# Two in-projection chunks between the opening's transposes, and the recurrent result kept in the decay buffer

## The chip, the cores and the metric

The kernel runs on one core of a Trainium2 chip. A core has a matrix engine (PE), a vector engine (DVE), a scalar engine (ACT), GpSimd (POOL) and SP, which here only issues transfers. ACT issues transfers too. Each engine works through its own instructions in order and waits on semaphores for the others. PE writes to PSUM, which has 8 banks of 512 float32 for each of 128 partitions. The metric is the device time of one execution in microseconds; lower is better.

## What is computed

One inference step of a hybrid decoder layer: 2048 prompt rows with 16 learned rows ahead of them, and 8 sample rows with a paged cache. Both groups go through

```python
h = rmsnorm(x, norm_mix)
q, k, v, f_logit, xr, gr = split(h @ w_in)          # 512, 512, 512, 8, 512, 512 columns
att = forgetting_attention(q, k, v, log_sigmoid(f_logit + b_forget))
rnn = linear_recurrence(conv4(xr), gates) * gelu(gr)
x = x + concat(rmsnorm(att), rmsnorm(rnn)) @ w_out
x = x + (gelu(conv3(g)) * val) @ w_ffn_down          # g, val = split(rmsnorm(x) @ w_ffn_up)
y = rmsnorm(x)
```

The change touches the first two lines and the order in time of the fourth. All arithmetic stays as it is.

## The kernel before, in words

The 2072 rows, padded to 2080, stand along the free dimension: activations are kept transposed. Products of full precision are made of three passes, high part by high part, high by low and low by high.

**The opening** takes 17 tiles of 128 rows (the last has 32). SP loads a tile into `xin[:, t % 2]` (L467). ACT takes the mean square (`mean_square`, L876 and L878). DVE scales the tile into `hn[:, t % 2]` (`normalise`, L1306 and L1308). PE transposes both, eight 128 x 128 pieces of the raw tile and eight of the normalised one (`turn`, L1838), into four banks; even tiles have banks 0 to 3, odd ones 4 to 7. ACT copies the raw half to `xst`, the normalised half to `XH` (`empty`, L886 and L887) and stores `xst` to `xT` in DRAM (L889). DVE subtracts to get the low part `XL` (`low`, L1315). Then small vector and scalar work on recurrent constants (L1351 to L1366) runs before `g_ev` is raised by 5, for which the first projection waits.

The semaphores of the opening: `x_tp` counts tiles transposed, `x_ev` evictions by ACT (two a tile), `x_sq` mean squares, `x_hn` normalised tiles, `x_lo` low parts. The load of tile t + 2 waits for `x_tp` of tile t, since it takes the same `xin` slot. The order on DVE is `normalise(t + 1)`, `low(t)`.

**The projections** take 21 chunks of 128 output columns: weights `WR` (SP, L477) are split by POOL into `WH` and `WL` (`split_w`, L706 and L708), and PE makes, per chunk, five blocks of 416 rows (`project`, L1857), block j into bank j, of 8 x 3 = 24 matmuls. DVE copies a bank to `ZS[:, j]` (`empty_block`, L1371) and ACT stores it (`store_block`, L918). Chunks 0 to 7 are xr and gr in turn, in four passes of a loop; chunk 8 holds the forget logits; then four groups of q, k and v follow, two in each pass of a loop over i.

**The recurrent branch** runs beside each group c of q, k and v. ACT loads `RX` from `xrT` (L985) once the previous store of `RX` to `mixT` has landed (`r_st`). DVE makes the convolution into `RC` between the evictions of q (L1448 to L1463); PE needs it for the gate products in chunk k (L1928, L1929). ACT writes the decay `RA` by block, DVE scans into `RW`, and the result of the group goes to `RX` (L1505), from where it is stored (L1040).

## Time and profile before

| | us |
|---|---|
| median of 3 runs | 3661.2 |
| range of the 3 runs | 3655.61 to 3663.19 |
| span of the profiled execution | 3658.3 |
| opening, to the first projection matmul | 110.07 |
| projections, to about | 690 |

The profile gives no device time of its own execution beside the span, so the span stands for it; it lies within the range of the three runs. In the page, a row of the chain says what the end was waiting for, followed backwards; a timeline row is start, duration, engine, line, what is written from what; "xN" merges N instructions. PE is the chain's engine in most of the span, so idle time of other engines costs nothing unless PE waits for them.

### The profile page before, as it was taken

To read this page: it belongs to the slowest core of one execution; us is meant where nothing else is said; L and a number is where in the kernel's file an instruction comes from. 1 tells how busy PE (TensorE), PEld (TensorE's weight loads), DVE (VectorE), ACT (ScalarE), POOL (GpSimd) and SP (SyncE) were. 2 spreads that over 40 slices of the span, in tenths; PEclk is the share of its full clock that TensorE was granted. 3 is DMA by queue.
4 is the path that set the end of the run, shared out by engine and by line. 5 is a ranking of instruction groups with operands and counts; after the bars stand their busy time and mean duration, and the time that the engine had idled before them with its cause. 6 is when DMAs were issued, how large, how long until landed. Compare 5 with 4: busy or idle time off the path is not lost.

```text
span 3658.3 us, 47526 instructions
## 1 busy us (share of the span) xinstructions
PE 3277.7 (90%) x15540; PEld 2765.0 (76%) x15540; DVE 1544.5 (42%) x1934; ACT 743.8 (20%) x1226; POOL 1024.5 (28%) x443
## 2 busy tenths in 40 slices
PE   4898989677898898999689899999999997999998
PEld 4898888543344444444589899999999997999998
DVE  4213333387656765672431644444444443112220
ACT  5000222321122122222300400000000002333332
POOL 1111111141332333230432622222222221444443
PEclk8999999767889988999899999999999998999999
DMA  5212444547565755563423311111111113544553
GB/s 186 77 70 64 100 93 97 109 105 203 172 175 172 211 153 163 165 197 94 127 95 124 116 47 46 46 46 46 49 46 46 46 41 124 168 162 164 189 180 108
DMA packets 254855, 422.68 MB, mean 116 GB/s; under 512 B 48545, under 2 KB 158730, under 8 KB 250554
## 3 DMA queue, kind: packets, MB, share of 16 engines
q1 hardware_dynamic: 168466, 326.84, 30.0%
q10 hardware_dynamic: 85936, 92.82, 8.4%
q8 instruction: 76, 1.25, 0.1%
q14 instruction: 89, 0.73, 0.1%
q0 software_dynamic: 288, 1.05, 0.1%
HBM read 337.35 MB, written 83.40 MB: 115 GB/s over the span
## 4 chain that ended last, share of the span: by engine, by line
PE 69%; DVE 8%; DMA 7%; issue 6%; SPq 4%; POOL 4%; ACT 2%; DVEq 0%; ACTq 0%; POOLq 0%
PE PS L2105 32%; PE PS L1857 12%; PE PS L2033 4%; PE PS L2044 3%; PE PS L2188 3%; PE PS L2190 3%; PE PS L2189 3%; DMA Kpg<-in_cache_k 2%; SPq L509 2%; DMA GR<-gT 2%; SPq L510 1%; PE PS L1956 1%; PE PS L2017 1%; DVE prod L1563 1%; POOL ML L835 1%
## 5 line engine op out<-in xcount | busy, mean ns | idle before, releaser
L2105 PE MATMUL PS<-MH,VH 128*128 128x416 f32 x2080 | 738.3, 355 | 35.9 <-issue 27.0
L2105 PE MATMUL PS<-MH,VL 128*128 128x416 f32 x2080 | 732.1, 352 | 0.0
L2105 PE MATMUL PS<-ML,VH 128*128 128x416 f32 x2080 | 732.0, 352 | 0.0
L2105 PEld LDWEIGHTS PS<-MH,VH 128*128 128x128 f32 x2080 | 392.8, 189 | 44.0 <-issue 27.9
L2105 PEld LDWEIGHTS PS<-ML,VH 128*128 128x128 f32 x2080 | 393.9, 189 | 3.8
L2105 PEld LDWEIGHTS PS<-MH,VL 128*128 128x128 f32 x2080 | 392.7, 189 | 5.1
L2033 PE MATMUL PS<-PT,VA 128*128 128x416 f32 (+16 forms) x816 | 354.3, 518 | 14.6 <-ACT PT L1097 13.3
L2188 PE MATMUL PS<-GH,DH 128*128 128x416 f32 x880 | 320.2, 364 | 46.9 <-POOL DL L860 28.5
L823 POOL TENSOR_TENSOR VR<-VR,gains 128x1024 f32<-128x1024 f32 x52 | 98.7, 1899 | 927.9 <-PE PS L2105 808.0
L860 POOL TENSOR_TENSOR DL<-DR,DH 128x1408 fp32r<-128x1408 f32 x80 | 258.3, 3229 | 353.3 <-ACT DH L1220 353.1
L1097 ACT ACTIVATE PT<-PS 128x416 f32<-128x416 f32 (+16 forms) x408 | 187.2, 460 | 718.4 <-PE PS L2019 501.6
L1956 PE MATMUL PS<-KA,QA 68*128 68x512 f32 (+3 forms) x360 | 218.3, 630 | 121.5 <-DVE MP L1524 89.8
L1857 PE MATMUL PS<-XH,WH 128*128 128x416 f32 x840 | 307.1, 366 | 19.2 <-issue 11.2
L2190 PE MATMUL PS<-GH,DL 128*128 128x416 f32 x880 | 313.6, 356 | 0.0
L2189 PE MATMUL PS<-GL,DH 128*128 128x416 f32 x880 | 313.4, 356 | 0.0
L1857 PE MATMUL PS<-XH,WL 128*128 128x416 f32 x840 | 296.9, 353 | 0.0
L1857 PE MATMUL PS<-XL,WH 128*128 128x416 f32 x840 | 296.4, 353 | 0.0
L1524 DVE TENSOR_REDUCE MP<-PS 128x1 f32<-128x512 f32 (+3 forms) x360 | 208.1, 601 | 132.7 <-PE PS L1956 96.8
L2044 PE MATMUL PS<-Vpg,sc 128*8 128x512 f32 x512 | 254.9, 622 | 3.4 <-DMA Vpg<-in_cache_v 3.1
L1766 DVE COPY GP<-PS 128x416 f32<-128x416 f32 x110 | 64.9, 592 | 423.0 <-PE PS L2105 422.6
L767 POOL TENSOR_TENSOR prod<-Kpg,qb 128x1024 f32<-128x1024 f32 x56 | 132.7, 2370 | 367.9 <-DMA Kpg<-in_cache_k 267.0
L1186 ACT ACTIVATE GC<-GC 128x416 f32<-128x416 f32 x110 | 60.8, 552 | 841.2 <-DVE GC L1738 754.1
(238 smaller groups left out, 4702.0 us busy)
## 6 DMA issues: line engine op xcount, KB each, us to landing
Kpg<-in_cache_k SPq DMA_DIRECT2D x256, 256.0 KB, 3.0
Vpg<-in_cache_v SPq DMA_DIRECT2D x256, 256.0 KB, 3.0
DR<-in_w_down SPq DMA_DIRECT2D x80, 704.0 KB, 4.1
gT<-GO ACTq DMA_DIRECT2D x110, 208.0 KB, 1.9
GR<-gT SPq DMA_DIRECT2D x55, 416.0 KB, 5.1
VR<-in_w_up SPq DMA_DIRECT2D x44, 512.0 KB, 3.5
Kst<-kT SPq DMA_DIRECT2D x24, 520.0 KB
WR<-in_w_stream SPq DMA_DIRECT2D x21, 512.0 KB, 3.5
```

Of the source, the lines that this page charges most:

```text
L767: e.tensor_tensor(prod[:, g % 2], Kpg[:, g % 4], qb[:, v].unsqueeze(1).to_broadcast([P, 2, DATT]), ALU.mult).then_inc(kpp, 1)
L860: e.tensor_tensor(DL[:, h], DR[:, h], DH[:, h].bitcast(F32), ALU.subtract).then_inc(d_lo, 1)
L1097: e.activation(PT[0:kr, t % 3, 0:n], PS[0:kr, (u + t) % 2, 0:n], ACT.Exp, scale=0.125).then_inc(ex, 1)
L1524: e.tensor_reduce(MP[0:rows, qt, pc:pc + 1], PS[0:rows, 2 + p % 2, 0:n], AX.X, ALU.max).then_inc(mx, 1)
L1857: mm = e.matmul(PS[:, j, 0:BW], w[:, u, k], x[:, k, cols(j)], start=(k == 0 and q == 0), stop=(k == KC - 1 and q == 2))
L1956: mm = e.matmul(o[:, 0:n], QA[0:HD + 4, v, qt * P:qt * P + rows], KA[0:HD + 4, v, k0:k0 + n], start=True, stop=not diag)
L2033: e.matmul(PS[:, 4 + (u + j) % 2, o:o + n], VA[0:kr, u, kt], PT[0:kr, t % 3, 0:n], start=(kt == 0), stop=t in ENDS).then_inc(pv, 1)
L2044: mm = e.matmul(PS[0:NH, 7, :], sc[:, u, 2 * g + m, :], Vpg[:, g % 4, m], start=(g == 0 and m == 0), stop=False)
L2105: mm = e.matmul(PS[:, j, 0:BW], w[:, u, k], x[:, k, cols(j)], start=(k == 0 and q == 0), stop=(k == KC - 1 and q == 2))
L2188: e.matmul(PS[:, v, 0:BW], DH[:, h, k], GH[:, r, m], start=(kk == 0), stop=False)
L2189: e.matmul(PS[:, v, 0:BW], DH[:, h, k], GL[:, r, m], start=False, stop=False)
L2190: e.matmul(PS[:, v, 0:BW], DL[:, h, k], GH[:, r, m], start=False, stop=(kk == FC - 1))\
```

## The change

The opening is written out as a list, `OPENING`: tiles 0 to 16, with ten units of work between and after them. A unit is one block of chunk 0 (even k) or chunk 1 (odd k), block j = k // 2. Units 0 and 1 follow tiles 4 and 5, units 2 and 3 tiles 7 and 8, and so on; units 8 and 9 follow tile 16. Units use banks 0 to 3 in turn, so every tile's raw transposes go to banks 4 and 5 and the normalised ones to banks 6 and 7; `x_tp` now counts halves. SP stores the units' blocks. The rest of the projections starts with chunk 2. `ZS` moves to an address of its own. In the recurrent branch the result is written over the decay `RA` and stored from there; the load of `RX` waits for the previous result to be computed, and the first write of `RA` in a group for the store to have landed.

```diff
@@ -162,6 +162,26 @@
     return plan
 
 
+def opening():
+
+    ready = {4: 0, 7: 1, 10: 2, 13: 3, 16: 4}
+    found, due = [], []
+    for t in range(NT):
+        found.append(("tile", t))
+        if due:
+            found.append(("unit", due.pop(0)))
+        if t in ready:
+            found.append(("unit", 2 * ready[t]))
+            due.append(2 * ready[t] + 1)
+    return found + [("unit", k) for k in due]
+
+
+def tiles_for(k):
+
+    return min(NT, ((k // 2 + 1) * BW + P - 1) // P)
+
+
+OPENING = opening()
 PLANS = [attention_plan(True, False), attention_plan(False, False), attention_plan(False, True)]
 
 
...
@@ -461,17 +481,25 @@
             e.dma_start(xin[:, 1], a["x_prompt"][0][P - NMETA:2 * P - NMETA, :]).then_inc(x_ld[1], 16)
             for u in range(2):
                 e.dma_start(WR[:, u], a["w_stream"][u]).then_inc(w_ld[u], 16)
-            with e.Fori(0, 7) as i:
-                for v in range(2):
-                    e.wait_ge(x_tp, 2 * i + v + 1)
-                    e.dma_start(xin[:, v], a["x_prompt"][0][bass.ds((2 * i + 2 + v) * P - NMETA, P), :])\
-                        .then_inc(x_ld[v], 16)
-            e.wait_ge(x_pad, 1)
-            e.dma_start(xin[0:NMETA, 0], a["x_prompt"][0][SEQ - NMETA:SEQ, :]).then_inc(x_ld[0], 16)
-            e.dma_start(xin[NMETA:NMETA + NS, 0], a["x_sample"][:, 0, :]).then_inc(x_last, 16)
-
-
-            with e.Fori(1, 10) as i:
+            for what, n in OPENING:
+                if what == "tile" and n < NT - 3:
+                    e.wait_ge(x_tp, 2 * n + 2)
+                    e.dma_start(xin[:, n % 2], a["x_prompt"][0][(n + 2) * P - NMETA:(n + 3) * P - NMETA, :])\
+                        .then_inc(x_ld[n % 2], 16)
+                if what == "tile" and n < 2:
+                    e.wait_ge(w_lo, n + 1)
+                    e.dma_start(WR[:, n], a["w_stream"][2 + n]).then_inc(w_ld[n], 16)
+                if what == "tile" and n == NT - 3:
+                    e.wait_ge(x_pad, 1)
+                    e.dma_start(xin[0:NMETA, 0], a["x_prompt"][0][SEQ - NMETA:SEQ, :]).then_inc(x_ld[0], 16)
+                    e.dma_start(xin[NMETA:NMETA + NS, 0], a["x_sample"][:, 0, :]).then_inc(x_last, 16)
+                if what == "unit":
+                    j = n // 2
+                    e.wait_ge(g_ev, 5 + n + 1)
+                    e.dma_start((xrT if n % 2 == 0 else grT)[0:P, cols(j)], ZS[:, n % NB]).then_inc(z_st[n % NB], 16)
+
+
+            with e.Fori(2, 10) as i:
                 for u in range(2):
                     e.wait_ge(w_lo, 2 * i + u - 1)
                     e.dma_start(WR[:, u], a["w_stream"][2 * i + u]).then_inc(w_ld[u], 16)
...
@@ -700,7 +728,9 @@
             def split_w(n, use, u):
 
                 e.wait_ge(w_ld[u], 16 * use + 16)
-                if not (isinstance(n, int) and n < 2):
+                if isinstance(n, int) and n in (2, 3):
+                    e.wait_ge(g_mm, n + 7)
+                elif not (isinstance(n, int) and n < 2):
                     e.wait_ge(g_mm, 5 * n - 5)
                 e.sem_inc(go, 1)
                 e.tensor_copy(WH[:, u], WR[:, u]).then_inc(w_hi, 1)
...
@@ -879,14 +911,15 @@
                              scale=1.0 / DM).then_inc(x_sq, 1)
 
             def empty(t, u, st, rows=P):
-                e.wait_ge(x_tp, t + 1)
+                e.wait_ge(x_tp, 2 * t + 1)
                 e.wait_ge(x_st[u], st + 1)
-                raw = PS[:, 4 * u:4 * u + 2, :].rearrange("p a (k n) -> p (a k) n", n=P)
-                nrm = PS[:, 4 * u + 2:4 * u + 4, :].rearrange("p a (k n) -> p (a k) n", n=P)
+                raw = PS[:, 4:6, :].rearrange("p a (k n) -> p (a k) n", n=P)
+                nrm = PS[:, 6:8, :].rearrange("p a (k n) -> p (a k) n", n=P)
                 e.activation(xst[:, u, :, 0:rows], raw[:, :, 0:rows], ACT.Copy).then_inc(x_ev, 1)
-                e.activation(XH[:, :, bass.ds(t * P, rows)], nrm[:, :, 0:rows], ACT.Copy).then_inc(x_ev, 1)
+                e.wait_ge(x_tp, 2 * t + 2)
+                e.activation(XH[:, :, t * P:t * P + rows], nrm[:, :, 0:rows], ACT.Copy).then_inc(x_ev, 1)
                 e.wait_ge(x_ev, 2 * t + 1)
-                e.dma_start(xT.rearrange("(k p) n -> p k n", p=P)[:, :, bass.ds(t * P, rows)],
+                e.dma_start(xT.rearrange("(k p) n -> p k n", p=P)[:, :, t * P:t * P + rows],
                             xst[:, u, :, 0:rows]).then_inc(x_st[u], 16)
 
             e.wait_ge(c_pool, 3)
@@ -894,18 +927,15 @@
             mean_square(0, 0, 16)
             mean_square(1, 1, 16)
             empty(0, 0, 0)
-            with e.Fori(0, 7) as i:
-                act0.start(i, 2)
-                for v in range(2):
-                    e.wait_ge(x_hn, 2 * i + v + 1)
-                    mean_square(2 * i + 2 + v, v, 16 * i + 32)
-                    empty(2 * i + 1 + v, 1 - v, 16 * (i + v))
-                act0.stop(7)
-            e.wait_ge(x_last, 16)
-            e.wait_ge(x_hn, 15)
-            mean_square(16, 0, 16 * 9, TAIL)
-            empty(15, 1, 16 * 7)
-            empty(16, 0, 16 * 8, TAIL)
+            for t in range(1, NT):
+                if t + 1 < NT:
+                    e.wait_ge(x_hn, t)
+                    if t + 1 == NT - 1:
+                        e.wait_ge(x_last, 16)
+                        mean_square(t + 1, 0, 16 * 9, TAIL)
+                    else:
+                        mean_square(t + 1, (t + 1) % 2, 16 * ((t + 1) // 2 + 1))
+                empty(t, t % 2, 16 * (t // 2), P if t < NT - 1 else TAIL)
             e.wait_ge(c_pool, 14)
             e.dma_start(rh0[:, :, 0:NS], a["rnn_h"]).then_inc(c_ld, 16)
 
...
@@ -981,7 +1014,7 @@
-                    e.wait_ge(r_st, 16 * c + 1)
+                    e.wait_ge(r_y, c + 1)
...
@@ -1014,6 +1047,7 @@
+                            e.wait_ge(r_st, 16 * c + 1)
...
@@ -1037,7 +1071,7 @@
-                            e.dma_start(mixT[bass.ds(DATT + c * P, P), :], RX[:, 3:3 + TP]).then_inc(r_st, 16)
+                            e.dma_start(mixT[bass.ds(DATT + c * P, P), :], RA[:]).then_inc(r_st, 16)
...
@@ -1301,8 +1335,8 @@
 
             def normalise(t, u, rows=P):
                 e.wait_ge(x_sq, t + 1)
-                if not (isinstance(t, int) and t < 2):
-                    e.wait_ge(x_tp, t - 1)
+                if t >= 2:
+                    e.wait_ge(x_tp, 2 * t - 2)
                 e.reciprocal(st0[0:rows, u, 2:3], st0[0:rows, u, 1:2]).then_inc(d0, 1)
                 e.wait_ge(d0, t + 1)
                 e.scalar_tensor_tensor(out=hn[0:rows, u], in0=xin[0:rows, u], scalar=st0[0:rows, u, 2:3],
@@ -1310,21 +1344,24 @@
 
             def low(t, u, rows=P):
                 e.wait_ge(x_ev, 2 * t + 2)
-                nrm = PS[:, 4 * u + 2:4 * u + 4, :].rearrange("p a (k n) -> p (a k) n", n=P)
-                c = bass.ds(t * P, rows)
+                nrm = PS[:, 6:8, :].rearrange("p a (k n) -> p (a k) n", n=P)
+                c = slice(t * P, t * P + rows)
                 e.tensor_tensor(XL[:, :, c], nrm[:, :, 0:rows], XH[:, :, c].bitcast(F32),
                                 ALU.subtract).then_inc(x_lo, 1)
 
             normalise(0, 0)
             normalise(1, 1)
-            low(0, 0)
-            with e.Fori(0, 7) as i:
-                for v in range(2):
-                    normalise(2 * i + 2 + v, v)
-                    low(2 * i + 1 + v, 1 - v)
-            normalise(16, 0, TAIL)
-            low(15, 1)
-            low(16, 0, TAIL)
+            e.sem_inc(g_ev, 5)
+            for what, n in OPENING:
+                if what == "tile":
+                    if n + 2 < NT:
+                        normalise(n + 2, n % 2, P if n + 2 < NT - 1 else TAIL)
+                    low(n, n % 2, P if n < NT - 1 else TAIL)
+                else:
+                    e.wait_ge(g_mm, n + 1)
+                    if n >= NB:
+                        e.wait_ge(z_st[n % NB], 16 + 1)
+                    e.tensor_copy(ZS[:, n % NB], PS[:, n % 4, 0:BW]).then_inc(g_ev, 1)
 
             g_steps = Steps(e, dv)
 
...
@@ -1362,15 +1399,15 @@
-            e.wait_ge(x_tp, NT)
+            e.wait_ge(x_tp, 2 * NT)
-            e.sem_inc(g_ev, 5)
-            with e.Fori(0, 4) as c:
+            e.wait_ge(t_pe, 2)
+            with e.Fori(1, 4) as c:
...
@@ -1502,7 +1539,7 @@
-                            e.tensor_tensor(x[:, 3:3 + TP], w[:], r[:], ALU.mult).then_inc(r_y, 1)
+                            e.tensor_tensor(al[:], w[:], r[:], ALU.mult).then_inc(r_y, 1)
...
@@ -1829,25 +1866,43 @@
             e.wait_ge(c_pool, 3)
 
             def turn(t, u, rows=P):
-                e.wait_ge(x_hn, t + 1)
-                if not (isinstance(t, int) and t < 2):
-                    e.wait_ge(x_ev, 2 * t - 2)
-                    e.wait_ge(x_lo, t - 1)
-                for src, b in ((xin, 4 * u), (hn, 4 * u + 2)):
+                for src, b in ((xin, 4), (hn, 6)):
+                    if b == 4 and t:
+                        e.wait_ge(x_ev, 2 * t - 1)
+                    if b == 6:
+                        e.wait_ge(x_hn, t + 1)
+                        if t:
+                            e.wait_ge(x_lo, t)
+                    else:
+                        e.wait_ge(x_sq, t + 1)
                     for k in range(KC):
                         mm = e.transpose(PS[:, b + k // 4, (k % 4) * P:(k % 4) * P + rows],
                                          src[0:rows, u, k * P:(k + 1) * P], identF[0:rows, 0:rows])
-                mm.then_inc(x_tp, 1)
-
-            turn(0, 0)
-            turn(1, 1)
-            with e.Fori(1, 8) as i:
-                for u in range(2):
-                    turn(2 * i + u, u)
-            turn(16, 0, TAIL)
-
-            e.wait_ge(x_ev, 2 * NT)
-            e.wait_ge(x_lo, NT)
+                    mm.then_inc(x_tp, 1)
+
+            def opening_unit(k):
+
+                j, u = k // 2, k % 2
+                tiles = tiles_for(k)
+                e.wait_ge(x_ev, 2 * tiles)
+                e.wait_ge(x_lo, tiles)
+                e.wait_ge(w_lo, u + 1)
+                if k >= 4:
+                    e.wait_ge(g_ev, 5 + k - 3)
+                for c in range(KC):
+                    for q, (w, x) in enumerate(((WH, XH), (WH, XL), (WL, XH))):
+                        mm = e.matmul(PS[:, k % 4, 0:BW], w[:, u, c], x[:, c, cols(j)],
+                                      start=(c == 0 and q == 0), stop=(c == KC - 1 and q == 2))
+                mm.then_inc(g_mm, 1)
+
+            for what, n in OPENING:
+                if what == "tile":
+                    turn(n, n % 2, P if n < NT - 1 else TAIL)
+                else:
+                    opening_unit(n)
+            e.wait_ge(g_ev, 5 + 9)
+            e.transpose(PS[0:TAIL, 5, 0:P], ZS[:, 8 % NB, 3 * P:BW], identF[:]).then_inc(t_pe, 1)
+            e.wait_ge(g_ev, 5 + 10)
 
             def project(n, u, j, hi, lo, w_hi_t, w_lo_t):
 
```

## Rows read from the trace of the kernel before

**Rows 1.** the page, part 4: the chain that ended last, by engine

```profile
PE 69%; DVE 8%; DMA 7%; issue 6%; SPq 4%; POOL 4%; ACT 2%; DVEq 0%; ACTq 0%; POOLq 0%
```

**Rows 2.** chain of waits in order of time, opening: start us, us, what

```profile
18.50 3.67 DMA xin<-in_x_prompt
...
25.52 3.63 PE PS L1838 x16
...
29.34 3.85 DMA xin<-in_x_prompt
```

**Rows 3.** timeline, first tiles: start us, us, engine, line, operation

```profile
14.64 1.94 PE L1838 MATMUL PS<-identF,xin 128*128 128x128 f32 x8 [14.64 <-DVE hn L1308]
...
22.19 1.06 ACT L876 ACTIVATE sqj<-xin 128x1024 f32<-128x1024 f32 x1 [1.92 <-DMA xin<-in_x_prompt]
...
24.00 1.28 DVE L1308 SCALAR_TENSOR_TENSOR hn<-xin,st,gmix 128x1024 f32<-128x1024 f32 x1
24.47 1.01 ACT L887 ACTIVATE XH<-PS 128x1024 f32 x1
...
25.65 1.22 DVE L1315 TENSOR_TENSOR XL<-PS,XH 128x1024 f32 x1 [0.37 <-ACT XH L887]
...
29.85 1.04 PE L1838 MATMUL PS<-identF,hn 128*128 128x128 f32 x8
```

**Rows 4.** timeline, the last two tiles

```profile
94.38 0.95 POOL L713 MEMSET xin<- 32x1024 f32 x1 [75.69 <-PE PS L1838]
...
98.17 1.05 ACT L876 ACTIVATE sqj<-xin 32x1024 f32<-32x1024 f32 x1 [1.79 <-DMA xin<-in_x_sample]
...
103.43 0.38 ACT L887 ACTIVATE XH<-PS 128x256 fp32r<-128x256 f32 x1
...
103.84 0.42 DVE L1315 TENSOR_TENSOR XL<-PS,XH 128x256 fp32r<-128x256 f32 x1 [1.12 <-ACT XH L887]
```

**Rows 5.** timeline, matmuls 1 and 13 of the first projection block

```profile
110.07 0.72 PE L1857 MATMUL PS<-XH,WH 128*128 128x416 f32 x1 [6.96 <-DVEq L1367]
...
114.35 0.35 PE L1857 MATMUL PS<-XH,WH 128*128 128x416 f32 x1
```

**Rows 6.** chain of waits in order of time, projections and recurrent branch

```profile
184.98 45.32 PE PS L1857 x240
...
415.76 14.97 DMA mixT<-RX
430.89 5.66 DMA RX<-xrT
```

**Rows 7.** timeline around the first recurrent boundary

```profile
407.37 0.59 DVE L1371 COPY ZS<-PS 128x416 f32<-128x416 f32 x1
...
414.59 2.40 POOL L708 TENSOR_TENSOR WL<-WR,WH 128x1024 fp32r<-128x1024 f32 x1
...
418.86 0.53 ACTq L971 DMA_DIRECT2D out_v_sample<-TS  x1
```

**Rows 8.** windows: stretch, its length, engines' busy us, PEclk, DMA share, GB/s

```profile
37.00:48.00 11.00, 6.76 (x34) 6.53 (x34) 5.45 (x7) 6.05 (x10) 0.00 (x0) 0.66 0.63 193
...
429.00:431.00 2.00, 1.00 1.00 389
431.00:433.00 2.00, 1.00 0.95 264
433.00:435.00 2.00, 1.00 1.04 438
```

**Rows 9.** PE's waits at the three boundaries: total us, times, longest

```profile
PE PS L1921 <- DVE ZS L1371: 7.4, 1, 7.4
...
PE PS L1857 <- issue: 11.2, 1, 11.2
...
PE PS L1921 <- DVE ZS L1371: 5.6, 1, 5.6
```

**Rows 10.** the instructions on xin: their transfers, issue to landing

```profile
DMA to landing us min/median/max: 2.0/4.0/5.1
```

More of the change, by code:

```diff
@@ L216, in build @@
         WL = sb("WL", [P, 2, KC, P], F32R, m1)
+        ZS = sb("ZS", [P, NB, BW], F32, m1)
         m0 = ExitStack()
@@ L224, in build @@
         m0.close()
-        ZS = sb("ZS", [P, NB, BW], F32, m1)
         TS = sb("TS", [P, 2, 4, P], F32, m1)
@@ L711, in _ @@
             split_w(1, 0, 1)
-            e.wait_ge(x_tp, 15)
+            e.wait_ge(x_tp, 30)
             e.memset(xin[0:TAIL, 0], 0.0).then_inc(x_pad, 1)
@@ L717, in _ @@
             e.wait_ge(x_ev, 2 * NT)
+            split_w(2, 1, 0)
             e.wait_ge(x_st[0], 16 * 9 + 1)
@@ L720, in _ @@
             e.memset(gw[:], 0.0).then_inc(c_gw, 1)
-            with e.Fori(1, 10) as i:
+            split_w(3, 1, 1)
+            with e.Fori(2, 10) as i:
                 for u in range(2):
@@ L925, in take_tail @@
                 e.wait_ge(t_ev, ev + 2)
-            with e.Fori(0, 4) as c:
+            take_tail(0, 0, 0)
+            e.dma_start(out["rnn_conv_prompt"][0, 0][:, 0:P], TS[NMETA - 3:NMETA, 0, 0]).then_inc(t_st[0], 16)
+            e.dma_start(out["rnn_conv_sample"][0][:, 2, 0:P], TS[NMETA:NMETA + NS, 0, 0]).then_inc(t_st[0], 16)
+            with e.Fori(1, 4) as c:
                 for j in range(NB):
@@ L1371, in empty_block @@
                 return e.tensor_copy(ZS[:, j], PS[:, j, 0:BW]).then_inc(g_ev, 1)
-            with e.Fori(0, 4) as c:
+            e.wait_ge(t_pe, 2)
+            with e.Fori(1, 4) as c:
                 for u in range(2):
@@ L1866, in chunk @@
                         after(j)
-            with e.Fori(0, 4) as c:
+            with e.Fori(1, 4) as c:
                 chunk(2 * c, 0)
```

## The prediction

> **What bounds the kernel now.** I began with the page: the chain that ended last lies on the matrix engine (PE) for 69% of the span [rows 1]. PE work that is neither added nor removed can only be moved, so what the change can win is PE's idle time near the edited places. I then read the chain of waits in order of time over the opening [rows 2] and the timeline of two of its tiles [rows 3]. The reader should see a loop two tiles long: PE transposes both tiles (3.6 to 3.7 us), the next input load starts 0.2 us after that and takes 3.67 and 3.85 us, squares and the normalised copy follow, and 10.84 us after the one load the next of its kind starts (18.50, 29.34). The transposes of seventeen tiles end at about 103.1, just before the last evictions [rows 4]. Then small vector work holds the first matmul until 110.07 [rows 5]. Third, I read the projection stage: 240 matmuls in 45.32 us with no gap [rows 6], and at the recurrent branch's boundaries the chain and the waits [rows 6, 9].
>
> **Part 1, the moved projections.** Chunks 0 and 1 are ten units of 24 matmuls, 45.32 us by a later pair [rows 6], so 4.53 us each. The first 12 intervals from 110.07 take 4.28 us [rows 5] against 12 x 0.19 = 2.3 later, so the pair ends and chunk 2 starts at about 110.07 + 45.3 + 2.0 = 157.4 today. That moment is what I compare. If the opening kept its pace, eight of the ten units would vanish into it, with the 7 us of small vector work.
>
> It does not keep it. The edit gives units the four lower banks, so all tiles share one pair of banks for raw and one for normalised transposes. PE's normalised half of tile t now waits for `low(t-1)` (x_lo >= t). On the vector queue `low(t-1)` is now written behind `normalise(t+1)`. That waits for tile t+1's square on the scalar engine, hence for its load, and the load waits for both halves of tile t-1 on PE. In the old order two tiles shared each turn of that circle. Now each tile goes round alone:
> - end of PE's half to start of the square: 0.19 (29.15 to 29.34), a load of 3.8, the mean of seven such in the chain, of which two stand in [rows 2]: 3.98 us;
> - start of the square to end of the normalised copy: 22.19 to 25.28, 3.09 us [rows 3];
> - `low`: 1.22 us, and 0.1 us until PE starts [rows 3];
> - eight normalised transposes: 1.04 us at the full clock, 1.9 us at the lower level, as after the pauses of some 5 us [rows 3].
>
> That is 9.43 us per tile at the full clock (warm), 10.30 at the lower (cold), in place of 10.9 / 2 = 5.45. The raw half is off this circle: it only needs the previous raw eviction.
>
> What the units cost: unit and raw half take 4.53 + 1.04 = 5.6 us, up to 7.6 where 2.0 us of slow start come in, and PE has 8.39 us in each circle until `low` is done. So they are hidden. After a unit the pause is under 3 us and I take the next half as warm; after a tile with no unit the pause is some 6 us and I take it as cold, like [rows 3]. Tiles 5, 6, 8, 9, 11, 12 and 14 are then warm, and 1 to 4, 7, 10, 13 cold.
>
> The moved queue work: the ten block stores go from the scalar queue to SP's, each issued before the next input load. Their wait (eviction, behind `low`) ends while PE does its half, so the issue delays the load by nearly nothing, but 208 KB stand in front of it; at 389 to 438 GB/s [rows 8] that is 0.5 us, for seven of the loads. Two weight loads move into tiles 0 and 1, 512 KB beside input loads: 0.5 us once. The scalar order (square of t+1, then evictions of t) hides its evictions behind the load. Vector evictions of units (0.59 us [rows 7]) fall between `low` and the next square's arrival.
>
> The sum of times: the first normalised half starts at 14.64 and takes 1.9, so tile 0 ends at 16.6. Tile 1: + 10.3 + 0.5 = 27.4. Tiles 2 to 4: + 30.9 = 58.3. Tiles 5 to 14: 7 x 9.43 + 3 x 10.30 = 96.9, and 7 x 0.5 for stores: 158.7. Tile 15 waits for the short last load by way of the pad: 94.33 to 98.17 is 3.84 [rows 4], the copy's end 3.0 later, `low` and PE 2.36: 167.9. Tile 16 needs only the eviction and `low` of tile 15: 0.15 + 1.02 + 0.1 + 1.22 + 0.1 + 1.04 = 3.6, 171.5. Its own eviction and `low`, 0.38 + 0.42 with the gaps 0.9 [rows 4], free unit 8 at 172.4. Units 8 and 9: 9.1; the last eviction and its signals 0.8: chunk 2 starts at 182.3. Its weights (split once unit 8 is done at 177: 2.40 us for the low part [rows 7] and under 2 for the high) are ready by 181. Against 157.4 this is a **loss of 24.9 us**. The small vector work of 3.7 us follows beside chunk 2, whose first eviction is due 4.5 us after its start, at no cost.
>
> Bounds: the circle's load has 3.67 us at least in the chain and 5.1 at most to landing [rows 2, 10]: -2 to +15 us over 14 circles. All halves warm: -6; all cold: +6. If a unit ran at the slow pace throughout (24 x 0.35 by [rows 5], + 1.94 for the raw half = 10.3 us), it would overrun 8.39 by 2.0, over eight units and the last two +24. No cost of the stores: -4.
>
> Here a rule speaks against my sum. What the row shows is two tiles of transposes back to back, 3.63 us, for one wait for a load [rows 2]. The Trainium skill (TensorE: Matmul & The Clock Gate, "HAM oscillation — how this bites in real kernels") reports that double-buffering PSUM gave no further gain to one kernel; by that, losing it costs nothing, and the time is that of the rival "kept pace" below.
>
> **Part 2, the recurrent result in the decay buffer.** Today the load of RX waits until the store of RX to mixT has landed: 14.97 us, then 5.66 us [rows 6]. PE stands 7.4 us at the first such boundary and 5.6 at the third, for evictions that stand behind the convolution, which needs RX [rows 9]. At the second PE stands for 11.2 us in "issue" [rows 9], which is no wait for RX, and no stall for RX follows: nothing to win. After the change the load is issued at about 419.4, behind the last value rows [rows 7], but on the same queue behind the same 1040 KB store. I take it as running after the store at the window's pace, mean of 389, 264 and 438 = 364 GB/s [rows 8]: 1.065 MB in 2.9 us, landing at 433.7 in place of 436.5. That saves 2.8 us; twice, **5.6 us**. Bounds: nothing, if the store is slowed by what the load takes; or the whole 7.4 + 5.6 = 13.0 us, if the load passes the store. I stay near the low end since store and load are equal in bytes and share the engines. The Trainium skill (DMA: Bandwidth & Descriptors, "Queues, rings and completion order") says each engine takes a queue's descriptors in ring order; the sum would be the same. The new wait, that the decay buffer's store has landed before the next exponentials, stands on the scalar queue ahead of everything behind it, but those exponentials need the convolution, so RX, which lands after the store even in the sum above: free.
>
> **Total.** 3658.3 + 24.9 - 5.6 = 3677.6 for the span; the median of the runs shown is 2.9 above this span, so 3680.5 us.
>
> **The rivals.**
> - *Kept pace* (faster). If `normalise(t+1)` were ready before PE ends tile t-1's half, the circle would be open and the opening would end at 103.1 as now. Unit 8 would start at 104.0, and chunk 2 at 104.0 + 9.1 + 0.8 = 113.9: 43.5 + 5.6 = 49 us less, 3612. It decides from the point at which load, square and copy (7.1 us) fit into one tile's period of 5.45; the load alone takes 3.67 or more after PE [rows 2], which speaks against it. For it speaks only that the lower bound of each term is not proven in the new rhythm.
> - *Light circle* (no change). Loads at 3.67 (-4), all halves warm (-6), no cost of stores (-4), and RX passing the store (-7.4): 3680.5 - 21 = 3659. Each is possible; together they are rare.
> - *Units not hidden* (slower still). PE pauses in every circle, and the granted clock in the opening is 0.66 at 37 to 48 [rows 8]. If units run at the lower level, 24 us more: 3704.
> - *The change does nothing for RX*, as ring order and slowed store cancel: 3686; inside the forecast's range.
>
> **How the numbers follow.** Circle per tile with units hidden, 0.72 (its own range 3668 to 3698); units not hidden or instruction fetch in the long unrolled code 0.12; light circle 0.09; kept pace 0.07. Leaving out kept pace and the far ends, the range is 3664 to 3704. 0.2% is 7.3 us, about what a measurement of this kernel can tell from no change. Faster 0.08; same 0.10 (light circle and the low tail of the forecast); slower 0.82.
>
> **What would show it.** Right: PE's groups of eight normalised transposes about 9.5 to 10.3 us apart, input loads issued singly at that spacing, `low` starting at the end of the normalised copy of the tile two ahead, unit 9 ending near 181, and the RX load landing near the store's landing plus 3. Wrong, if tiles follow at 5.5 us (the circle is open), if a unit and raw half last over 8.4 us, or if RX lands before 430 and PE's boundary stalls vanish.

## The result

| | before | after |
|---|---|---|
| median of the runs (5 each), us | 3662.91 | 3684.69 |
| range of the runs, us | 3655.61 to 3666.07 | 3674.43 to 3688.69 |
| span of the profiled execution, us | 3658.3 | 3682.9 |
| ratio after to before, 95% interval | | 1.0054 (1.0037 to 1.007) |

The changed kernel is slower by 0.54%, or 21.8 us between the medians; the spans differ by 24.6 us. The forecast was 3680.5 in a range of 3664 to 3704. To see whether it was right for its reasons, the same eight places of both traces are set against each other. Each is the start of the same piece of work, or the landing of the same transfer.

| place | before | after | difference | forecast |
|---|---|---|---|---|
| tile 14's halves done on PE | – | 161.0 | – | 158.7 |
| chunk 2 starts | 157.5 | 187.65 | +30.1 | +24.9 |
| last projection evicted, POOL writes Kst | 690.1 | 724.4 | +34.3 | +19.3 |
| first Kst load landed | 720.1 | 755.0 | +34.9 | +19.3 |
| first block of attention's output, AO | 788.9 | 824.5 | +35.6 | +19.3 |
| last block of attention's output, AO | 1760.0 | 1787.3 | +27.3 | +19.3 |
| first load of the down product | 3066.3 | 3093.9 | +27.6 | +19.3 |
| end of the span | 3658.3 | 3682.9 | +24.6 | +19.3 |

The loss is older than the attention stage: it is +30 where the projections go on with chunk 2, a little more at their end, and some 10 less at the end of the span. So two questions stand open: why the recurrent part gave nothing of its 5.6 us, and where these 10 us came back from, in stages that the change doesn't touch.

The page of after, part 4, answers [rows 1]; the chain is by engine:

```profile
PE 64%; issue 10%; DVE 8%; DMA 6%; SPq 5%; POOL 4%; ACT 2%; ACTq 0%; DVEq 0%; POOLq 0%
```

PE has fallen from 69% to 64% of the chain and "issue" has risen from 6% to 10%. The rise is a single piece, in the chain of the opening of after (start us, us, what):

```profile
18.76 142.25 issue
```

This chain runs back from the last input load to the pad that POOL writes into `xin` before it, and from there along POOL's own queue, where 142.25 us, 3.9% of the span, read as "issue". By the waits POOL stood for PE all that time. So the shares of the chain say little about the opening, and the waits say more. Over the first 190 us of after (columns: engine, line, waited for, us in total, times, longest) the rows of POOL, DVE and PE are:

```profile
POOL xin L743 <- PE PS L1879: 142.3, 1, 142.3
DVE st L1340 <- ACT st L910: 121.6, 16, 11.6
...
PE PS L1879 <- DVE XL L1349: 74.2, 16, 7.7
```

In all sixteen tiles after the first PE waits for the low part of the tile before, 74.2 us together. Before, the transposes waited on the scalar engine's eviction in seven places and for `hn` in four.

The timeline of one turn in after (columns as in [rows 3]), from one normalised half to the next:

```profile
56.80 1.94 PE L1879 MATMUL PS<-identF,hn 128*128 128x128 f32 x8 [7.01 <-DVE XL L1349]
...
58.77 0.33 SPq L487 DMA_DIRECT2D xin<-in_x_prompt  x1
...
62.86 1.06 ACT L908 ACTIVATE sqj<-xin 128x1024 f32<-128x1024 f32 x1 [3.07 <-DMA xin<-in_x_prompt]
...
63.63 1.03 PE L1879 MATMUL PS<-identF,xin 128*128 128x128 f32 x8
...
64.57 1.29 DVE L1342 SCALAR_TENSOR_TENSOR hn<-xin,st,gmix 128x1024 f32<-128x1024 f32 x1
...
65.78 1.22 DVE L1349 TENSOR_TENSOR XL<-PS,XH 128x1024 fp32r<-128x1024 f32 x1
66.91 0.58 DVE L1364 COPY ZS<-PS 128x416 f32<-128x416 f32 x1
67.14 1.06 PE L1879 MATMUL PS<-identF,hn 128*128 128x128 f32 x8 [2.47 <-DVE XL L1349]
67.52 0.35 SPq L499 DMA_DIRECT2D xrT<-ZS  x1
...
68.23 0.33 SPq L487 DMA_DIRECT2D xin<-in_x_prompt  x1
```

Read it downwards. PE ends tile 4's half at 58.74 and the load of tile 6 goes out at once. The unit and tile 5's raw half fill PE until 64.66. The load lands, the square starts at 62.86, the normalised copy of tile 6 ends at 65.86, and only then does `low` of tile 4 run, although its data had lain ready since ACT's eviction ended at 59.8. PE's next half starts 0.14 us after `low`, at 67.14: 10.34 us after the last one. Over the whole opening the normalised halves of tiles 0 and 16 start at 14.63 and 173.82, 9.95 us per tile; before it was 5.45.

The end of the opening, chain of waits of after (start us, us, what):

```profile
162.36 2.73 DMA xin<-in_x_sample
...
175.83 10.86 PE PS L1894 x48
...
187.65 27.43 PE PS L1912 x144
```

### The profile page after: what moved, and what is told of

Same layout as the page of the kernel before. It is cut to its first block, busy times and chain, and to the rows that moved or that the text cites. A ratio compares the mean times of both kernels' runs of the same rounds, so it can differ in the third digit from the quotient of the medians.

```text
span 3682.9 us, 47256 instructions
## 1 busy us (share of the span) xinstructions
PE 3268.0 (89%) x15540; PEld 2759.3 (75%) x15540; DVE 1548.0 (42%) x1934; ACT 744.9 (20%) x1226; POOL 1025.2 (28%) x443
## 4 chain that ended last, share of the span: by engine, by line
PE 64%; issue 10%; DVE 8%; DMA 6%; SPq 5%; POOL 4%; ACT 2%; ACTq 0%; DVEq 0%; POOLq 0%
PE PS L2160 31%; PE PS L1912 10%; PE PS L2099 3%; PE PS L2088 3%; PE PS L2243 3%; PE PS L2245 3%; PE PS L2244 3%; DMA GR<-gT 2%; DMA Kpg<-in_cache_k 2%; SPq L537 2%; SPq L538 1%; DVE prod L1600 1%; PE PS L2011 1%; DVE MP L1561 1%; POOL ML L867 1%
## 5 line engine op out<-in xcount | busy, mean ns | idle before, releaser
L2243 PE MATMUL PS<-GH,DH 128*128 128x416 f32 x880 | 320.1, 364 | 44.1 <-POOL DL L892 26.5
L1912 PE MATMUL PS<-XH,WH 128*128 128x416 f32 x760 | 278.2, 366 | 14.1 <-issue 12.2
L1912 PE MATMUL PS<-XH,WL 128*128 128x416 f32 x760 | 268.1, 353 | 0.0
L1912 PE MATMUL PS<-XL,WH 128*128 128x416 f32 x760 | 267.9, 352 | 0.0
```

The lines of the kernel that those rows point to most:

```text
L1912: mm = e.matmul(PS[:, j, 0:BW], w[:, u, k], x[:, k, cols(j)], start=(k == 0 and q == 0), stop=(k == KC - 1 and q == 2))
L2243: e.matmul(PS[:, v, 0:BW], DH[:, h, k], GH[:, r, m], start=(kk == 0), stop=False)
```

## The experiments

All ratios are against runs of the kernel before on the same chip. Two theories about the opening stood against each other: the circle of the prediction, in which `low` stands behind `normalise` of the tile two ahead, and a cost of the single banks, the units or the instructions themselves. About the recurrent part there were two as well: the load gains its 2.8 us each time, or it gains nothing because the wait for the store never was what held it.

### One part at a time (e1, e2)

The changed kernel with the four edits of the recurrent branch taken back (e1, shown), and the kernel before with the same four made (e2, the reverse of these lines):

```diff
-                    e.wait_ge(r_y, c + 1)
+                    e.wait_ge(r_st, 16 * c + 1)
...
-                            e.wait_ge(r_st, 16 * c + 1)
...
-                            e.dma_start(mixT[bass.ds(DATT + c * P, P), :], RA[:]).then_inc(r_st, 16)
+                            e.dma_start(mixT[bass.ds(DATT + c * P, P), :], RX[:, 3:3 + TP]).then_inc(r_st, 16)
...
-                            e.tensor_tensor(al[:], w[:], r[:], ALU.mult).then_inc(r_y, 1)
+                            e.tensor_tensor(x[:, 3:3 + TP], w[:], r[:], ALU.mult).then_inc(r_y, 1)
```

> The changed kernel with its recurrent part taken back: RX is again loaded after the store of RX has landed; the new opening stays. In the trace of the changed kernel RX lands 20.9 us after the store to mixT is issued, against 20.8 before. Theory (the circle of one tile in the opening is the whole loss, the recurrent part brings nothing): the time of the changed kernel, 3685 us within 4. Rival (the recurrent part saves its 5.6 us and something else in that run ate them): about 3690 us.

Measured: 3684.05 us, ratio 1.0083 (1.006 to 1.0106).

> The kernel before with the recurrent part of the change alone. Theory (no gain, as RX still lands about 21 us after the store is issued and PE still stands 7.4 us at the first boundary): 3663 us, ratio 1.000. My recorded step (load right behind the store, 2.8 us at two boundaries): 3657 us, ratio 0.9985. If the load passed the store: 3650 us.

Measured: 3659.96 us, ratio 1.0013 (0.9999 to 1.0028). The opening alone carries the whole loss, and the recurrent part alone saves nothing: the 5.6 us of the forecast would be a ratio of 0.9985, which lies below the interval of e2. Against its own runs of before, though, e1 is 27.7 us slower and the whole change 21.8. That gap of 5.9 us is as large as the saving that was forecast; the two intervals overlap, so e1 by itself can't tell the theories apart. The chain of waits shows what became of the load. First the opening alone, where load follows store as in [rows 6], then the recurrent part alone:

```profile
445.29 14.64 DMA mixT<-RX
...
460.10 6.13 DMA RX<-xrT
```

```profile
420.34 15.16 DMA RX<-xrT
```

The wait for the store has gone from the chain, and the load, issued about 10 us earlier than in [rows 6], lasts 15.16 us instead of 5.66. It lands at 435.5, before at 436.55.

### The order of two instructions on the vector queue (e3)

The changed kernel, with `low` written ahead of `normalise` in the opening. Nothing else differs, banks and units least of all.

```diff
                 if what == "tile":
+                    low(n, n % 2, P if n < NT - 1 else TAIL)
                     if n + 2 < NT:
                         normalise(n + 2, n % 2, P if n + 2 < NT - 1 else TAIL)
-                    low(n, n % 2, P if n < NT - 1 else TAIL)
```

> The changed kernel with one edit: on the vector queue low(n) stands before normalise(n + 2) instead of behind it. Theory (that order closes the circle of 9.4 to 10.4 us per tile): the circle is open, a tile takes about 5 us, 6.6 with a unit on PE (4.53 + 2 x 1.04), so chunk 2 starts near 120 instead of 187.6 and the time is 3615 to 3625 us. Rival (single-banked PSUM or the transfers set the pace, whatever the vector order): tiles stay near 10 us and the time near 3685 us; one between them, if the single banks cost a part.

Measured: 3621.78 us, ratio 0.99 (0.9876 to 0.9924); chunk 2 starts at 127.60. That is 60 us earlier than in after and 30 earlier than before. In the waits over the first 190 us the row that stood at 74.2 has shrunk, and in the timeline `low` now starts well before the next normalised copy:

```profile
PE PS L1879 <- DVE XL L1349: 8.3, 10, 1.6
```

```profile
61.49 1.23 DVE L1349 TENSOR_TENSOR XL<-PS,XH 128x1024 fp32r<-128x1024 f32 x1 [0.34 <-ACT XH L920]
...
62.86 1.06 PE L1879 MATMUL PS<-identF,hn 128*128 128x128 f32 x8 [0.16 <-DVE XL L1349]
63.05 1.28 DVE L1342 SCALAR_TENSOR_TENSOR hn<-xin,st,gmix 128x1024 f32<-128x1024 f32 x1
```

The normalised halves of tiles 0 and 16 now start at 14.5 and 114.15: 6.2 us per tile, units included. PE now waits in seven places for the eviction of the raw half instead, 12.3 us in all. So the single banks by themselves cost at most the 0.8 us per tile between 6.2 and the 5.45 of before, with eight units inside; the order in which DVE takes two operations cost some 60 us. The chain of this kernel shows what is late next, the input loads on their own:

```profile
53.95 4.12 DMA xin<-in_x_prompt
...
65.26 4.70 DMA xin<-in_x_prompt
```

Of the 60 us that chunk 2 gained against after, the total shows the whole: e1, with the opening of after, took 3684.05 us on the same chip, 62.3 more.

### All units after the last tile (e4)

```diff
-    ready = {4: 0, 7: 1, 10: 2, 13: 3, 16: 4}
...
-    return found + [("unit", k) for k in due]
+    return [("tile", t) for t in range(NT)] + [("unit", k) for k in range(10)]
```

> The changed kernel with all ten units after tile 16 instead of eight of them between tiles. Theory (eight units are wholly hidden in PE's wait of 8.4 us in each circle): their 8 x 4.53 = 36 us come back, some 4 us for colder transposes are added and some 4 us of store cost saved: 3721 us. Rival (units are not hidden but lengthen the circles): nothing changes or little, 3685 to 3700 us.

Measured: 3715.09 us, ratio 1.0162 (1.0137 to 1.0187). Waits of PE over the first 190 us, and the chain:

```profile
PE PS L1870 <- DVE XL L1340: 104.9, 16, 7.4
```

```profile
177.18 48.03 PE PS L1885 x240
...
226.19 27.44 PE PS L1903 x144
```

Without units between the tiles, tile 16 is done at nearly the same time (the first unit starts 1.35 us later, 177.18 against 175.83), and chunk 2 starts 38.5 us later than in after (226.19 against 187.65). Eight units are 36 us of that. So in the circle they did cost nothing, as forecast: PE simply stood 30.7 us longer for the same sixteen low parts. The rival by which units were not hidden falls. The total shows 31.0 us of the 38.5 (3715.09 against 3684.05 of e1, on the same chip).

### The low part twice (e5)

`low` of tiles 0 to 14 is computed a second time into a scratch tile, before the real one; the wait of `normalise` is counted accordingly. This lengthens one link of the circle by a known amount and nothing else.

```diff
+                if t < NT - 2:
+                    e.tensor_tensor(dup[:], nrm, XH[:, :, c].bitcast(F32), ALU.subtract).then_inc(d0, 1)
                 e.tensor_tensor(XL[:, :, c], nrm[:, :, 0:rows], XH[:, :, c].bitcast(F32),
                                 ALU.subtract).then_inc(x_lo, 1)
```

> The changed kernel with every low part of tiles 0 to 14 computed twice (the first copy into a scratch tile; no result of the kernel depends on it). Theory (low stands in a circle that every tile goes round alone): each of 15 circles grows by one such operation, 1.13 to 1.22 us, so 17 to 18 us more than the changed kernel, about 3702 us against 3685. Rival (low is covered by the load or by PE's transposes and units): the changed kernel's time, 3685 us.

Measured: 3705.91 us, ratio 1.0112 (1.009 to 1.0135). Timeline of one turn, and the start of chunk 2 in the chain:

```profile
47.24 1.22 DVE L1351 TENSOR_TENSOR dup<-PS,XH 128x1024 fp32r<-128x1024 f32 x1
48.38 1.22 DVE L1352 TENSOR_TENSOR XL<-PS,XH 128x1024 fp32r<-128x1024 f32 x1
```

```profile
207.81 27.43 PE PS L1915 x144
```

Fifteen doubled operations of 1.14 us (48.38 less 47.24) are 17.1 us; chunk 2 came 20.2 us later, and the median is 21.2 above that of after. The 3 us beyond the 17.1 are not traced; two traces with the same opening, after and e1, have chunk 2 start 1.8 us apart (187.65 and 185.86). DVE is busy for 42% of the span of after, and yet what is put on this one operation arrives in full at the end. That is what it is to lie on the circle.

### What holds the load of RX (e6)

In the trace of after the store goes out at 447.11, the load at 453.39. The DMA queue of ACT around them (timeline), and the windows (stretch, length, then PE, PEld, DVE, ACT and POOL busy us, PEclk, DMA share, GB/s):

```profile
443.18 0.39 ACTq L1070 DMA_DIRECT2D out_rnn_h_sample<-RW  x1
...
447.11 0.76 ACTq L1074 DMA_DIRECT2D mixT<-RA  x1
...
453.39 3.71 ACTq L1018 DMA_DIRECT2D RX<-xrT  x1
```

```profile
453.00:455.00 2.00, 2.00 (x13) 1.98 (x12) 0.00 (x0) 0.00 (x0) 0.00 (x0) 1.00 1.67 51
...
461.00:463.00 2.00, 2.00 (x12) 1.98 (x12) 0.00 (x0) 0.00 (x0) 0.00 (x0) 1.00 0.98 401
```

For 12 us after the store's issue hardly anything moves: at 453 to 455 the share of the engines is 1.67, and yet they move only 51 GB/s, where at 461 to 463 a share of 0.98 moves 401. Then 1.06 MB of store, 1.06 MB of load and 0.52 MB of weights go at about 400 GB/s. The packets of three windows of after, 443 to 445, 453 to 455 and 461 to 463:

```profile
DMA packets 1236, 0.02 MB, mean 11 GB/s; under 512 B 1201, under 2 KB 1236, under 8 KB 1236
...
DMA packets 21, 0.10 MB, mean 51 GB/s; under 512 B 3, under 2 KB 9, under 8 KB 9
...
DMA packets 227, 0.80 MB, mean 401 GB/s; under 512 B 17, under 2 KB 83, under 8 KB 185
```

The share of 1.67 is not made of small pieces: it is 21 packets, most of them large, which last 2.5 us each (1.67 x 16 engines x 2 us over 21), where the 227 later ones last 0.14. The small pieces came before. Some 1200 packets start at 443 to 445, and they belong to two transfers issued ahead of the store: the last column of `RW` (prompt) and eight columns (samples) go to DRAM as 128 x 9 = 1152 elements of 4 bytes each. Between them and the store two transfers of value rows are issued, which are the other candidates. They stay as they are in what follows.

To test it the recurrent state is stored another way. PE transposes the nine columns into bank 6, ACT copies them, and they go out as nine rows of 512 bytes. The edit is made on the kernel before, with neither part of the change; the computed result is the same. It changes the place in the queue as well as the size of the pieces: the state now goes out behind the store to `mixT` and directly ahead of the load of `RX`.

```diff
+                        if j == 3:
+                            e.wait_ge(r_sc, c + 1)
+                            e.transpose(PS[0:1 + NS, 6, 0:P], RW[:, TPR - 1:TPR + NS], identF[:]).then_inc(x_pad, 1)
...
-                            e.dma_start(out["rnn_h_prompt"][0].rearrange("o n -> n o")[bass.ds(c * P, P), :],
-                                        RW[:, TPR - 1:TPR]).then_inc(r_ho, 16)
...
+                    e.activation(HR[0:1 + NS], PS[0:1 + NS, 6, 0:P], ACT.Copy).then_inc(d0, 1)
...
+                    e.dma_start(out["rnn_h_prompt"][0][:, bass.ds(c * P, P)], HR[0:1]).then_inc(r_ho, 16)
+                    e.dma_start(out["rnn_h_sample"][0][:, bass.ds(c * P, P)], HR[1:1 + NS]).then_inc(r_ho, 16)
```

> The kernel before, where the recurrent state is transposed on PE (one transpose a group, into bank 6) and stored as nine rows of 512 bytes, instead of 1152 elements of 4 bytes each. Theory (these small writes stand ahead of the store to mixT on the scalar queue and hold it for 10 of its 15 us, and hold instruction fetch at the second boundary): the store lands in about 5 us, RX in about 5 more, PE's stalls of 7.4, 11.2 and 5.6 us shrink to 0 to 3 each: 15 to 24 us faster than the kernel before, some 3637 us, ratio 0.9935 to 0.996. Rival (the store takes 15 us by itself, or by the value rows around it): 3658 us, ratio 1.000.

Measured: 3607.22 us, ratio 0.985 (0.9833 to 0.9867). The transfers around the first boundary, 410 to 440, in the trace of before and then in this kernel's (tiles, queue, KB each, us from issue to landing; ahead of them the packets by size):

```profile
DMA packets 3426, 3.60 MB, mean 120 GB/s; under 512 B 1672, under 2 KB 3040, under 8 KB 3168
...
mixT<-RX ACTq DMA_DIRECT2D x1, 1040.0 KB, 15.0
RX<-xrT ACTq DMA_DIRECT2D x1, 1040.0 KB, 5.7
WR<-in_w_stream SPq DMA_DIRECT2D x1, 512.0 KB, 16.7
```

```profile
DMA packets 2692, 4.24 MB, mean 141 GB/s; under 512 B 545, under 2 KB 2306, under 8 KB 2434
...
mixT<-RX ACTq DMA_DIRECT2D x1, 1040.0 KB, 4.4
RX<-xrT ACTq DMA_DIRECT2D x1, 1040.0 KB, 5.8
...
WR<-in_w_stream SPq DMA_DIRECT2D x1, 512.0 KB, 5.2
```

Some 1100 small packets are gone from the window, and with them 10.6 us of the store and 11.5 us of a weight load on another queue. So the 15 us of the "store" [rows 6] were 4.4 us of store and 10.6 us for which 4.5 KB ahead of it held it up. The place alone doesn't explain it: the nine rows now stand directly ahead of the load of `RX`, which took 5.8 us, as against 5.7. Whether the 4-byte writes, moved behind the store as they are, would have done less harm was not tried. This is the step that the prediction had wrong: the load of RX was not waiting for a store, both were waiting for what went before. PE's waits between 400 and 760, first the longest of before (its other two, for ZS and in "issue", stand in [rows 9]), then those with the rows:

```profile
PE PS L1956 <- POOL QA L743: 31.3, 1, 31.3
```

```profile
PE PS L1961 <- POOL QA L744: 22.2, 1, 22.2
...
PE PS L1857 <- issue: 3.4, 1, 3.4
```

The two stalls for ZS, 7.4 and 5.6 us, have gone; the one in "issue" has shrunk by 7.8 us, and the wait for the first load of attention by 9.1 (Kst lasts 12.55 us in the chain in place of 21.58). The projections end at 663.6, not 690.1; the stalls are 20.8 us of these 26.5, and much of the rest is PE's slow start behind them, as in the 29.98 us for the 144 matmuls after the second stall of before, against 27.44 for as many in e3 (from 127.60). The expectation was a gain of 0.4 to 0.65%; it was 1.5%. Of the 49 us between the two spans, 35.6 are there when Kst has landed. The rest lies in the attention stage, and its cause is open (below).

### Is the recurrent part worth something without the small writes? (e7)

The same edit with the recurrent part:

> The run before this one with the recurrent part of the change added (result into the decay buffer, RX loaded at once). Theory (with the small writes gone there is little left for RX to wait for, as the convolution keeps up with PE): within 3 us of the run before this one. Rival (the recurrent part pays once the queue is clear): 3 to 8 us below it.

Measured: 3611.66 us, ratio 0.9861 (0.9839 to 0.9883), against 0.985 (0.9833 to 0.9867) without it. The forecast was within 3 us of e6 and it came out 4.4 above, inside both intervals; a saving is not to be seen.

### All that helps, together (e8, e9)

The changed kernel with `low` first and with the state stored as rows; then the same with the recurrent part taken back, beside a second run of the first.

> The changed kernel with low(n) before normalise(n + 2) and the recurrent state stored as rows. The two gains lie in different stages, so they should add: -35 (measured for the vector order, against the kernel before) and -15 to -24: about 3602 us, ratio 0.984 to 0.986. If the gain of the rows only appears with the old opening: 3622 us.

Measured: 3586.43 us, ratio 0.9799 (0.9777 to 0.9822). Chunk 2 starts at 130.34. The expectation of 0.984 to 0.986 counted the rows at 15 to 24 us, where e6 had given 54. The two gains measured alone, 1.0% and 1.5%, would give 0.975; together they gave a little less, and why is open.

> The run with both gains, e8, with the recurrent part of the change taken back (result again into RX, the load of RX behind the landed store). Theory (the recurrent part brings nothing, with or without the small writes): within 0.2% of e8, ratio 0.978 to 0.982 to the kernel before. Rival (it is worth some us once the queue is clear): 3 to 8 us above e8, ratio 0.981 to 0.983.

Measured: 3597.24 us, ratio 0.9788 (0.9774 to 0.9802).

> The same kernel as e8 beside its counterpart without the recurrent part, for a direct comparison on one chip. Both theories: ratio 0.978 to 0.982 to the kernel before; the difference to the other run of this call is what counts.

Measured: 3592.54 us, ratio 0.9788 (0.9771 to 0.9804). With e9 this is the best version found, 2.0 to 2.1% below the kernel before. With and without the recurrent part the ratio is the same to four digits; the medians are 4.7 us apart, within the spread of either's runs. The recurrent part has now been measured in four surroundings (alone, with the new opening, with rows, with rows and `low` first), and in none do the intervals keep apart from nothing. They are some 5 to 8 us wide to each side, so a saving of 2 or 3 us would not show in them.

## Why the prediction was right, and where it was not

**The circle: right, and shown.** The waits are as drawn. The period was forecast at 9.43 to 10.30 us and is 9.95 on average; doubling one link (e5) moves the start of chunk 2 by 20.2 us for 17.1 added, and cutting the circle by exchanging two instructions (e3) frees 60 us. The rival *kept pace* and the *light circle* fall with it. *Kept pace* had the Trainium skill beside it (TensorE: Matmul & The Clock Gate, "HAM oscillation — how this bites in real kernels"), where double-buffering PSUM brought one kernel nothing. Carried over to this kernel, the trace disagrees: 9.95 us per tile with one set of banks, 5.45 with two. Once `low` went first, single banks ran at 6.2 us per tile with eight units inside, so the statement comes near the truth there. What decides is whether a bank's release stands behind something slow in its engine's queue.

**Units hidden: right, and shown** by e4, with 38.5 us for eight units and what starts slowly in them.

**The sum of the opening: 24.9 forecast, 30.1 measured.** The step that failed is "after a unit the pause is under 3 us and I take the next half as warm". The halves of tiles 6, 8, 12 and 15 followed pauses of 2.5 to 3.2 us and still took 1.94 us, the time at the lower level. Those of 5, 9, 11 and 14 took 1.06 us after pauses just as long. In the timeline of after, one of each:

```profile
138.82 1.94 PE L1879 MATMUL PS<-identF,hn 128*128 128x128 f32 x8 [3.21 <-DVE XL L1349]
...
159.89 1.06 PE L1879 MATMUL PS<-identF,hn 128*128 128x128 f32 x8 [3.01 <-DVE XL L1349]
```

In e1, with the same opening, it was again four of these eight, but others: tiles 9, 12, 14 and 15 (12 with 1.79 us), and chunk 2 started at 185.86. So which of them are slow differs between two executions of one opening, and with it a part of these 5 us.

In after, three such halves before tile 14's end are 3 x 0.9 = 2.7 us, which covers the 2.3 by which tile 14 ended late (161.0 against 158.7). Tile 15 came another 1.2 late: its half took 0.9 more, and the way from the pad to its neighbour's square 4.16 us (161.0 to 165.16) in place of 3.84. Units 8 and 9 took 10.86 us in place of 9.1: the slow start of PE, counted for today's first block [rows 5], had been left out for the last two units. Together that gives 2.3 + 1.2 + 1.8 = 5.3, against 5.2 by the table.

**The recurrent part: 5.6 forecast, nothing measured.** The step that failed is "I take it as running after the store at the window's pace [...] landing at 433.7". The load did go out earlier. Around the first boundary of after it landed 20.9 us after the store's issue, before 20.8. The "window's pace" of [rows 8] was real, but it is that of a backlog that drains, and the load could not join it any sooner. The store landed 0.8 us later than before, and the load 5.1 us after it where the prediction had 2.9. That the load comes behind the store issued ahead of it on the same queue agrees with the Trainium skill (DMA: Bandwidth & Descriptors, "Queues, rings and completion order"), by which each engine takes a queue's descriptors in ring order. The bound "nothing, if the store is slowed by what the load takes" held; the cause was a third transfer, which was in the trace of before all along, as two transfers of 8.5 and 16.2 us for 0.5 and 4 KB:

```profile
out_rnn_h_prompt<-RW ACTq DMA_DIRECT2D x1, 0.5 KB, 8.5
out_rnn_h_sample<-RW ACTq DMA_DIRECT2D x1, 4.0 KB, 16.2
```

That a 1040 KB store lasting 15 us runs at 71 GB/s, a sixth of the 438 in [rows 8] a little later, was the sign to ask what stood ahead of it. e6 shows the cause of the delay. That it also explains all of the missing 5.6 us doesn't follow: with the small writes gone (e7 against e6) the recurrent part brings nothing either. There RX is no longer awaited at all, since the ZS stalls that it could have shortened are gone.

**The new wait was free**, as said: the recurrent part cost nothing that shows in e2, in e7, or in e8 against e9 either.

**Boundaries.** Forecast at 5.6 us less, they came out at about 3 us more. PE's waits between 400 and 760 in after, against [rows 9] with 7.4, 11.2 and 5.6:

```profile
PE PS L1976 <- DVE ZS L1407: 15.2, 2, 7.8
PE PS L1912 <- issue: 12.2, 1, 12.2
```

**The last stages.** The forecast had nothing happen after the projections, and +34 there became +24.6 at the end. Some 8 us of it came back between the first and the last head of attention. From the first block of AO to the first load of the stage behind attention, one execution each of before and of the kernels up to e8 took between 956.4 (e6) and 973.9 us (before); after took 965.6. Single heads differ by as much: from its first block of AO to that of the next head, the fifth took 128.8 us before, 121.5 after, 117.9 in e6. The code is the same in all. A part of that spread is a property of the execution and not of the kernel: from the first to the last block of AO the same kernel took 965.1 us in the trace of e8 and 959.5 in that of its second run, where before took 971.1, after 962.8 and e1 954.9. So one trace each can't show that these 8 us belong to the change, and their cause stays open. The nearness of 3680.5 to 3684.7 is partly luck: 5.2 us too little in the opening and 5.6 + 3 + 1 at the boundaries and in the rest of the projections were offset by 10 that no step had foreseen.

## What to carry to other kernels

Before two sets of buffers become one, write down for each buffer who fills it, who frees it, and what stands ahead of the freeing instruction on its engine's queue. A release written behind an instruction that waits for a load closes a circle through the load, and here the remedy was to swap two lines: from +0.5% to -1.0%. And before a wait for a transfer is removed, divide its bytes by its time: where the pace is far below what the queue does a moment later, look for small elements ahead of it, for they may be what is being waited for. They need not be in the window where the time goes: here they had all started two to four us before the store was issued.

## What the runs showed of the hardware

1152 writes of 4 bytes, 4.5 KB in all and four times in the kernel, held up 1040 KB behind them by 10.6 us and a 512 KB load on another queue by 11.5 us. The 1200 small packets start within 2 us; what lasts are the landing of the transfer (16.2 us for 4 KB) and the large packets that follow (2.5 us each, later 0.14). As nine rows of 512 bytes a time the kernel lost 1.5% of its time. They also lengthened a stall of PE that the profile calls "issue" (11.2 us against 3.4), and a load of attention that comes after the last of them (21.58 against 12.55 us). The other traces agree: the stall is 8.6 to 12.2 us in the seven kernels with these writes and 3.1 to 3.6 in the five traces without, the load 20.4 to 22.1 and 12.1 to 12.7. How they get at "issue" is not shown. In before the stall runs from 507.1 to 518.3, and one packet of the kind "instruction" starts in it (DMA view, 507 to 508):

```profile
q8 instruction: 1, 0.02, 22.9%
```

That is 3.7 us of one engine; in e6 the packet at this place takes 8.2% of such a window, 1.3 us. So instructions do come in more slowly there. But the packet ends some 7 us before the stall does, so it is at most a part of the cause.

The transposes' pace after a pause is not settled by the pause alone: after 2.5 to 3.2 us without work they ran at the lower level four times in eight, with the same unit of matmuls before the pause. In e1, with the same opening and pauses of 1.1 to 3.1 us at these places, it was four in eight again, at other tiles.
